# The state-space mixer of a three-block model: another order of its steps on four engines, and a product and a square moved to another engine

## The reference

```python
# layer 1: a selective state-space mixer (8 groups of 4 heads), then an MLP; layer 2: latent attention, MLP;
# then a block with neighbourhood attention, a short convolution and an MLP. Only this mixer is touched:
def ssd_mixer(h, w_in, conv_w, conv_b, dt_bias, a_log, d_skip, norm_g, w_out):
    zxbcdt = h @ w_in
    z, xbc, dt = jnp.split(zxbcdt, [SSD_D_INNER, SSD_D_INNER + SSD_CONV_DIM], axis=-1)
    xbc = jax.nn.silu(causal_depthwise_conv(xbc, conv_w, conv_b))
    xs, b_in, c_in = jnp.split(xbc, [SSD_D_INNER, SSD_D_INNER + SSD_GROUPS * SSD_STATE], axis=-1)
    dt = jax.nn.softplus(dt.astype(f32) + dt_bias.astype(f32))
    ...
    decay = jnp.exp(jnp.where(causal, a_cs[..., :, None] - a_cs[..., None, :], -jnp.inf))
    cb = jnp.einsum('bclgn,bcsgn->bcgls', c_c, b_c)
    y_diag = jnp.einsum('bcgjls,bcsgjp->bclgjp', cb[:, :, :, None] * decay, xdt)
    ...
    y = y + xs.astype(f32) * jnp.repeat(d_skip.astype(f32), SSD_HEAD_DIM)
    g = (y * jax.nn.silu(z.astype(f32))).reshape(bsz, L, SSD_GROUPS, SSD_D_INNER // SSD_GROUPS)
    g = g * lax.rsqrt(jnp.mean(g * g, axis=-1, keepdims=True) + EPS)
    g = g.reshape(bsz, L, SSD_D_INNER) * norm_g.astype(f32)
    return g.astype(h.dtype) @ w_out
```

## Time and profile before

| | us |
|---|---|
| median of three runs | 1168.44 (1166.44 to 1171.82) |
| the profiled execution | 1166.44 |
| its span, first to last instruction | 1164.8 |
| PE busy in the span | 1116.0 (96%) |
| DVE / ACT / POOL busy | 780.0 / 668.3 / 161.3 |
| granted clock of PE, mean | 0.991 |

### The profile page before, as it was taken

One profiled execution on the slowest core, in us unless ns is written; L12 is line 12 of the kernel. 1 busy time (PEld: TensorE's weight loads), 2 busy tenths in 40 slices (PEclk: granted clock), 3 DMA queues, 4 the chain that ended last, 5 costly groups with the idle time before them and its releaser, 6 DMA issues.

```text
span 1164.8 us, 23763 instructions
## 1 busy us (share of the span) xinstructions
PE 1116.0 (96%) x8898; PEld 1072.4 (92%) x8898; DVE 780.0 (67%) x1127; ACT 668.3 (57%) x1063; POOL 161.3 (14%) x122
## 2 busy tenths in 40 slices
PE   6999999999999999689889999999999999999998
PEld 5889999899999999567679999999998999999998
DVE  4699999778665454578757665555687577666453
ACT  5799889455554444388745555445454756555332
POOL 0344444317000001200011000000001202000000
PEclk9999999999999999999899999999999999999999
DMA  5555445475555555232225555655544555555552
GB/s 207 175 171 176 165 163 163 143 224 176 167 175 166 183 174 163 91 109 91 73 70 192 189 181 181 190 176 190 167 145 145 165 180 183 194 183 182 189 188 90
DMA packets 53225, 190.32 MB, mean 163 GB/s; under 512 B 5920, under 2 KB 7072, under 8 KB 53168
## 3 DMA queue, kind: packets, MB, share of 16 engines
q1 hardware_dynamic: 51408, 182.95, 48.0%
q0 software_dynamic: 1760, 6.59, 1.8%
HBM read 188.44 MB, written 1.08 MB: 163 GB/s over the span
## 4 chain that ended last, share of the span: by engine, by line
PE 87%; DVE 7%; ACT 3%; issue 2%; DMA 0%; SPq 0%; ACTq 0%; DVEq 0%
PE lin L412 27%; PE lin L414 26%; PE lin L413 26%; DVE w_lo L1218 2%; ACT w_hi L835 1%; PE ps L505 1%; DVE cv L1297 1%; PE lin L643 1%; PE lin L645 1%; ACT pr L1106 1%; PE ps L445 0%; ACT pr L1145 0%; PE ps L484 0%; PE ps L492 0%; DVE lat L1487 0%
## 5 line engine op out<-in xcount | busy, mean ns | idle before, releaser
L1218 DVE TENSOR_TENSOR w_lo<-w_raw,w_hi 128x1024 fp32r<-128x1024 f32 (+2 forms) x319 | 388.1, 1218 | 271.9 <-ACT w_hi L835 271.1
L835 ACT ACTIVATE w_hi<-w_raw 128x1024 fp32r<-128x1024 f32 (+1 forms) x343 | 355.4, 1040 | 241.5 <-PE lin L414 240.8
L412 PE MATMUL lin<-x_hi,w_hi 128*128 128x256 f32 (+1 forms) x1528 | 442.4, 290 | 13.1 <-DVE cv L1297 4.4
L414 PE MATMUL lin<-x_hi,w_lo 128*128 128x256 f32 (+1 forms) x1528 | 436.6, 286 | 0.0
L413 PE MATMUL lin<-x_lo,w_hi 128*128 128x256 f32 (+1 forms) x1528 | 435.7, 285 | 0.0
L412 PEld LDWEIGHTS lin<-x_hi,w_hi 128*128 128x128 f32 x1528 | 289.4, 189 | 17.2 <-DVE cv L1297 4.8
L413 PEld LDWEIGHTS lin<-x_lo,w_hi 128*128 128x128 f32 x1528 | 288.8, 189 | 1.4 <-issue 1.0
L414 PEld LDWEIGHTS lin<-x_hi,w_lo 128*128 128x128 f32 x1528 | 289.7, 190 | 0.0
L414 PE MATMUL lin<-hid_hi,w_lo 128*128 128x256 f32 (+1 forms) x768 | 218.2, 284 | 0.0
L413 PE MATMUL lin<-hid_lo,w_hi 128*128 128x256 f32 (+1 forms) x768 | 217.9, 284 | 0.0
L412 PE MATMUL lin<-hid_hi,w_hi 128*128 128x256 f32 (+1 forms) x768 | 217.4, 283 | 0.0
(11 more groups left out here) (251 smaller groups left out, 1495.9 us busy)
## 6 DMA issues: line engine op xcount, KB each, us to landing
w_raw<-w SPq DMA_DIRECT2D x343, 512.0 KB, 3.3
acs_bc<-acs_dram POOLq DMA_DIRECT2D x8, 544.0 KB, 4.8
bias_mask<-rpb POOLq DMA_DIRECT2D x4, 512.0 KB, 10.1
h<-h SPq DMA_DIRECT2D x4, 272.0 KB, 3.5
out<-h SPq DMA_DIRECT2D x8, 128.0 KB, 3.1
cst<-const SPq DMA_DIRECT2D x1, 784.0 KB, 8.7
vecs<-vec SPq DMA_DIRECT2D x1, 131.5 KB, 2.3
acs_dram<-y POOLq DMA_DIRECT2D x1, 34.0 KB, 2.4
```

The source lines that it names most:

```text
L412: mm3(o, wh, xh, start=first and i == 0, stop=False)
L414: ins = mm3(o, wl, xh, start=False, stop=last and i == kts - 1)
L835: a(w_hi[pg.slot][:, 0:n], w_raw[pg.slot][:, 0:n], ACT.Copy).then_inc(w_hi_done, pages)
L1218: tt(w_lo[pg.slot][:, 0:n], w_raw[pg.slot][:, 0:n], w_hi[pg.slot][:, 0:n].bitcast(F32), ALU.subtract)\
```

## The change

PE does the transposes of x before the products of C and B. ACT rounds both pages of chunk C first, then computes the decays; the rounding of the first page of the next A comes ahead of the first sigmoid, the sigmoid of z behind it; the logs and the second sigmoid change places; and ACT takes over the squares of y2. DVE no longer computes y2, does the mask behind the scaled tokens instead of ahead of the convolution, and w_lo of the next A ahead of the product xs. POOL computes y2 instead of its squares, and issues the broadcast behind its first w_lo.

```diff
--- before.py
+++ after.py
@@ -517,8 +517,8 @@
                 if has_lin and not first:
                     lin_chunk(c, k, T)
                 if has_scan:
+                    x_transposes(s + (-1))
                     cb_products(s + (-1))
-                    x_transposes(s + (-1))
                 if has_lin:
                     lin_chunk(c + 1, k + 1, T)
                 if first:
@@ -931,37 +931,38 @@
             def slot(s, has_lin=True, has_scan=True, has_stat=True):
                 c = s.times(3, C_GRP)
                 g, gs = s + (-1), s + (-2)
+                if has_lin:
+                    hi((c + 2).page(0))
+                    hi((c + 2).page(1))
                 if has_scan:
                     decay(g, 0)
                     decay(g, 1)
+                if has_stat:
+                    act.wait_ge(y2_done, (gs + 1).value)
+                    a(h_sq[:, 0:2, :], y2[:, :, :], ACT.Square).then_inc(ysq_done, 1)
+                if has_lin:
+                    conv0(s, 0)
+                    hi((c + 3).page(0))
+                    act.wait_ge(clamped, s.times(2, 1).value)
+                    sigmoid(sg[:, 0:2, :], sg_step, s.times(6))
+                if has_scan:
                     kz = g.times(3, K_GRP + 2)
                     act.wait_ge(drained[kz.parity], kz.half + 1)
                     sigmoid(z_sg[:, :, :], zg_step, g.times(3), z_raw[:, :, :])
                 if has_lin:
-                    hi((c + 2).page(0))
-                    conv0(s, 0)
-                    hi((c + 2).page(1))
-                if has_lin:
-                    if s.base:
-                        decay_logs(s, 0)
-                    act.wait_ge(clamped, s.times(2, 1).value)
-                    sigmoid(sg[:, 0:2, :], sg_step, s.times(6))
-                    hi((c + 3).page(0))
                     conv0(s, 1)
                     hi((c + 3).page(1))
                 if not has_lin:
                     hi2(s + (C_SOUT - 6))
+                if has_lin and s.base:
+                    decay_logs(s, 0)
                 if has_stat:
                     act.wait_ge(gstat_done, (gs + 1).value)
                     a(g_ln[:, :], ps5[:, 0:T], ACT.Ln, bias=eps_t[:, 0:1], scale=1.0 / 256).then_inc(gln_done, 1)
                     act.wait_ge(gln_done, (gs + 1).value)
                     a(g_inv[:, :], g_ln[:, :], ACT.Exp, scale=-0.5).then_inc(ginv_done, 1)
                 if has_lin:
-                    if s.base:
-                        decay_logs(s, 1)
                     hi((c + 4).page(0))
-                    act.wait_ge(clamped, s.times(2, 2).value)
-                    sigmoid(sg[:, 2:4, :], sg_step, s.times(6, 3))
                 if has_stat:
                     act.wait_ge(y3_done, (gs + 1).value)
                     for q in range(2):
@@ -969,9 +970,11 @@
                         a(g_hi[:, t.value, :], z_s[gs.parity][:, q, :], ACT.Copy, scale=v((t + V_SNORM).value))\
                             .then_inc(gh_done, 1)
                 if has_lin:
+                    act.wait_ge(clamped, s.times(2, 2).value)
+                    sigmoid(sg[:, 2:4, :], sg_step, s.times(6, 3))
                     if not s.base:
                         decay_logs(s, 0)
-                        decay_logs(s, 1)
+                    decay_logs(s, 1)
                     hi((c + 4).page(1))
 
             slot(At(0), has_scan=False, has_stat=False)
@@ -1353,9 +1356,6 @@
                         dve.wait_ge(y_done, gs.times(2, q + 1).value)
                         stt(y1[:, q, :], xs_s[gs.parity][:, q, :], v(gs.times(2, V_DSKIP + q).value),
                             (ps6, ps7)[q][:, 0:T], ALU.mult, ALU.add).then_inc(y_read, 1)
-                    dve.wait_ge(y_read, gs.times(2, 2).value)
-                    dve.wait_ge(z_silu_done, (gs + 1).value)
-                    tt(y2[:, :, :], y1[:, :, :], z_s[gs.parity][:, :, :], ALU.mult).then_inc(y2_done, 1)
                 if has_scan:
                     if g.base == 0:
                         dve.wait_ge(cols_done, 4)
@@ -1365,22 +1365,19 @@
                     dve.wait_ge(gl_done, gs.times(2).value)
                 if has_lin:
                     lo((c + 2).page(0))
-                    if has_scan:
-                        causal_cb(g)
                     conv(s, 0)
                     clamp(sg[:, 0:2, :], cv[:, 0:2, :]).then_inc(clamped, 1)
                 if first:
                     dt_columns()
                 if has_scan:
                     scaled_tokens(g)
-                    if not has_lin:
-                        causal_cb(g)
+                    causal_cb(g)
                     dve.wait_ge(cbm_done, (g + 1).value)
                     head_mix(g, 0)
                     head_mix(g, 1)
                 if has_lin:
+                    lo((c + 3).page(0))
                     silu(s, 0, xs_s[s.parity][:, :, :], cv[:, 0:2, :], sg[:, 0:2, :])
-                    lo((c + 3).page(0))
                     conv(s, 1)
                     clamp(sg[:, 2:4, :], cv[:, 2:4, :]).then_inc(clamped, 1)
                 if has_scan:
@@ -1765,17 +1762,20 @@
 
             def slot(s, has_lin=True, has_stat=True):
                 c, gs = s.times(3, C_GRP), s + (-2)
-                if has_lin and s.base:
-                    acs_rows(s)
                 if has_stat:
 
-                    pool.wait_ge(y2_done, (gs + 1).value)
-                    tt(h_sq[:, 0:2, :], y2[:, :, :], y2[:, :, :], ALU.mult).then_inc(ysq_done, 1)
+                    pool.wait_ge(y_read, gs.times(2, 2).value)
+                    pool.wait_ge(z_silu_done, (gs + 1).value)
+                    if gs.base:
+                        pool.wait_ge(y3_done, gs.value)
+                    tt(y2[:, :, :], y1[:, :, :], z_s[gs.parity][:, :, :], ALU.mult).then_inc(y2_done, 1)
                     pool.wait_ge(ysq_done, (gs + 1).value)
                     tt(y_sum[:, :], h_sq[:, 0, :], h_sq[:, 1, :], ALU.add).then_inc(ysum_done, 1)
                 if has_lin:
 
                     lo((c + 2).page(1))
+                    if s.base:
+                        acs_rows(s)
                     lo((c + 3).page(1))
                     lo((c + 4).page(1))
 
```

## The result

| | before | after |
|---|---|---|
| median of the runs | 1168.84 us (1166.44 to 1171.82) | 1183.85 us (1181.22 to 1185.12) |
| profiled execution / span | 1166.44 / 1164.8 | 1182.7 / 1181.0 |
| granted clock, mean | 0.991 | 0.986 |

The changed kernel takes 1.0125 of the time before, interval [1.0095, 1.0153]: some 15 us more, where +9.9 was forecast on the profiled execution and 1177.5 for the median. The median before is that of four runs.

The account below looks back on a forecast made before the run. PE bound the slots at 22.6 us, DVE without slack; -1.4 at slot 2, +11.0 for five turns and +0.3 behind made +9.9 us, 1176.3 from the profiled 1166.44; predicted median 1177.5, range 1169 to 1182.

Parts of the forecast that it names:

- The turn: Slots 2 to 7: one serial turn takes 24.8 us where PE needs 22.6, so PE waits 2.2 a slot.
- Zero to Square: From the start of ACT's last rounding of the slot before to its Square, which waits for POOL's y2: 5.75 us.
- Square to zero: From ACT's Square to the start of its last rounding in that slot, waits included: 19.05 us.
- y2 alone: Price of y2 on POOL, shown by no row: between 1.05 and 1.4 us, taken as 1.05.
- rival 1: POOL's y2 is not held up by DVE's w_lo: turn 23.75, +3.6 us, 1170 to 1172; chance 0.22.
- the point on which it turns: PE's group sum waits for DVE's mask cbm, now behind convolution, clamp and scaled tokens; sum may begin 6.0 us after Square.
- The front: Slots 0 and 1: chunk C of slot 1 starts about 3.1 us earlier; slot 2's group sum keeps 1.4 us.
- Rival 2: PE's waits bring the clock down: each fall costs 1.7 us, in six slots 10 more, 1187; chance 0.06.
- The tail: Behind slot 7, statistics of groups 6 and 7 run as before, y_sum in time; +0.3 us allowed.
- Rival 3: Order costs nothing, DVE perhaps spared its blocking: turn stays 22.6, only front's 3.1 us left, 1165; chance 0.14 with the like.

Follow-up runs that it names:

- decays first: Changed kernel with ScalarE's two decays again ahead of the two roundings of chunk C: 1176.29 us, ratio 1.0074 to the kernel before.
- second profile: The changed kernel run once more, unedited (also called the second measurement): 1180.98 us, ratio 1.0122 to the kernel before.
- the two edits together: Kernel before with both roundings of C ahead of decays and z's sigmoid, y2 on POOL, and Square on ACT ahead of z's sigmoid: 1174.27 us, ratio 1.0043.
- g_hi late: Changed kernel with g_hi issued behind the second pair of z sigmoids on ScalarE: 1175.82 us, ratio 1.0062 to the kernel before.
- y2 on DVE: Changed kernel with y2 on DVE again, behind y1, Square left on ACT: 1174.37 us, ratio 1.0059 to the kernel before.
- the mask early: Changed kernel with the mask (cbm) again ahead of the first convolution on VectorE: 1183.81 us, ratio 1.0143 to the kernel before.
- the kernel before with y2 on POOL: Kernel before with y2 on POOL and Square on ACT, behind the taps and second rounding: 1170.20 us, ratio 0.9996.
- the mask late: Kernel before with only the mask moved behind the scaled tokens on VectorE: 1168.03 us, ratio 0.9983.

## Why the prediction was right in kind and short in size

- **The turn.** Zero to Square was forecast 5.75 us and is 5.84; Square to zero 19.05 and is 19.0; the turn 24.8 and is 24.85. The steps inside agree too: POOL's w_lo from 1.13 (1.12), y2 held up by DVE's w_lo, g_hi waiting 0.6 (0.61), the group sum 6.0 behind the Square (5.91). One price was off without harm: y2 alone takes 1.35 us, not 1.05, close to the upper bound of 1.4. But held up it ends only 1.22 us behind DVE's w_lo, so that a small part of it runs ahead of the w_lo.
- **What it rested on** is confirmed by undoing: y2 being held up is worth 0.9 a turn (decays first), its place on POOL 1.1 with that 0.9 in it, the wait for y3 0.65. The first is rival 1's case, turn 23.75 by the forecast and 23.94 measured.
- **Parts alone.** The forecast put the loss on no single edit. The mask, which it called the point on which it turns, only names the wait: alone it costs nothing, and moving it back alone gains nothing.
- **The front.** -1.4 was forecast, -1.3 came, and so close an agreement is in part luck: the second profile of the same kernel has -2.2, and before's stretch holds a clock fall where after's has none. As forecast, of the 3.2 us gained by chunk C of slot 1 (58.73 less 29.07, against 60.17 less 27.27) over half went at once in the first wait of 2.18.
- **Step that failed: the terms beside the turn in the sum, and the kernel before from which it counts.** The mechanism was right; these were sized too small. The turns were put at +11.0 and made +12.5: 0.4 from turns of 24.9, and 1.1 from two clock falls. Rival 2 was given 0.06 as all or nothing, and left out of the sum; it came in two slots of six, at 0.4 and 0.7 us, and in the second profile again in two, at 1.9 and 0.4. The tail was put at +0.3 and made +1.35: in slot 8 ACT's Square waits 2.18 us for y2, so the roundings and g_hi come late, and the output projection is interrupted twice (rows at 235.08 and 240.25: 0.35 and 0.36 us idle, 0.5 each by the starts of the products). From the group sum of slot 8 to that of slot 9 it takes 13.88 us instead of 12.63. I had looked only at whether the sum's input was in time. Together 2.6 us, which makes +12.5 for the mixer and 1180.1 in place of 1177.5.
- **The rest of the miss.** That leaves 3.7 us to 1183.85, and 0.9 to the 1180.98 of the second measurement. The forecast put the kernel before at 1167.6 (1166.44, its shortest run, plus 1.2); beside the changed kernel its median was 1168.84, so 1.2 of the 3.7 belong there (its other medians were 1167.10, 1169.72 and 1170.15). The other 2.5 are in no part of the profiled mixer. Outside it the profiles show clock falls that come and go in both orders; whether the change has a part in them stays open.
- **Rival 3** is refuted: the turn is long because of the chain through ACT, with DVE 5 us idle in it.

## What to carry to other kernels

When several engines pass work round in a ring, write out the ring with starts and not busy times: its length against the bound engine's time decides, and edits that are free alone can stop being so together (here 0, 0, and then 0.5 us a turn, with the Square in another place than when it was free). Undo edits one by one from the changed kernel as well as doing them one by one on the old: the first shows the price in company, the second only the slack; and prices on one ring overlap, so that they are not to be added up. A wait's name is the place where the ring touches the bound engine; moving that step alone moves the wait. And a stretch with no turns behind it, as the first slots here, keeps its gain.

## What the runs showed of the hardware

- **Who goes first at the shared port.** In the changed kernel y2 pays 1.0 us for DVE's w_lo, which had waited since 98.63; with decays first y2, issued 0.19 us ahead, takes 1.37 and the w_lo 2.26. So far the Trainium skill's rule holds (SBUF — State Buffer, "Who interferes with whom": it is the order of issue that decides which engine is blocked). But in the kernel with the two edits together DVE's w_lo started first and y2 was not held up:

```profile
121.76 1.38 POOL L1778 TENSOR_TENSOR y<-y,z_s 128x544 f32<-128x544 f32 x1
...
121.63 2.60 DVE L1223 TENSOR_TENSOR w_lo<-w_raw,w_hi 128x1024 fp32r<-128x1024 f32 x1
```

  It was DVE's w_lo that was lengthened, from 1.22 to 2.60; by the rule on these starts it should be y2, to about 2.4. A start in the trace 0.13 us earlier doesn't say who has the port; at 222.09 in the kernel before, with 0.16, POOL was the one that waited. What makes the difference was not tried.
- **The clock and waits.** Of ten waits of PE of 1.9 to 2.6 us at group sums (in the changed kernel, twice, and with decays first or g_hi late) five were followed or accompanied by a fall to 1.2 GHz, of nineteen shorter ones in those kernels and with y2 on DVE none. That is no threshold: before, neither of the waits of 2.04 and 2.34 us brought one, and with the mask early the last of three waits of 1.5 to 1.6 us, a turn apart, did:

```profile
154.76 0.39 PE L412 MATMUL lin<-x_hi,w_hi 128*128 128x272 f32 x1 [1.64 <-DVE cv L1300]
```

  The granted clock was down from 155 to 159 there (mean 0.57). A fall of some 7 us began in the wait of 2.56 us above, and in waits of 2.91 and 3.32 us ahead of slot 1 (the kernel before with y2 on POOL, and with the mask late); yet one of 2.81 us with the mask early brought a fall of half that length. In the kernels that wait at the group sums a fall in the slots made the turns 0.3 to 1.9 us longer, of the 1.7 to 3.4 us of work that it took from PE, since the next waits absorbed the rest.
